# Copies of value pages into a DRAM scratch: all from SyncE beside the input projection, or shared out over SyncE and ScalarE and three stages

## What is computed

```python
for l in range(DEPTH):                        # 2
    h = x @ w_in                              # 1024 -> 2836 columns
    y_conv = conformer_conv(h_conv, ...)      # GLU, causal conv of width 31, LayerNorm, swish, pointwise
    y_pool = pool_mixer(h_pool, ...)          # causal window sums
    # past of the 8 decode sequences: 32 pages of 128 tokens each, rows [k_cmp, v_cmp, k_sel, v_sel]
    past = take(cache_nsa_kv[l, :, :, c], page_table)      # c = 0..3
    y_att = nsa_mixer(q, kv, gates, past, ...)             # compressed + selected + window branch
    y_gdn = gdn_mixer(...)                    # gated delta rule
    x1 = layer_norm(ALPHA * x + concat(...) @ w_out)
    x = layer_norm(ALPHA * x1 + square(relu(x1 @ w_up)) @ w_down)
```

## Time and profile before

| what | value |
|---|---|
| median of 3 runs | 3044.47 us |
| profiled execution, own time | 3055.84 us |
| its span | 3054.1 us |
| PE busy | 2617.3 us (86%) |
| DVE, ACT, POOL busy | 873.4, 568.4, 236.7 us |
| DMA queue q1 (SyncE's), share of 16 engines | 32.0% |
| DMA queue q10 (ScalarE's) | 1.2% |
| mean granted TensorE clock | 0.895 |
| copies into v_dram | 512 DMAs of 64 KB |

### The profile page before, as it was taken

The page is one execution under the profiler, slowest core; times in us unless marked ns, Lnnn a source line. Parts: engine busy times, 40 slices in busy tenths (PEclk is TensorE's granted clock), DMA queues, the critical chain, the costliest instruction groups (busy, mean ns, idle before and its releaser), DMA issues. The chain is left out here.

```text
span 3054.1 us, 44579 instructions
## 1 busy us (share of the span) xinstructions
PE 2617.3 (86%) x17428; PEld 2135.7 (70%) x17428; DVE 873.4 (29%) x1901; ACT 568.4 (19%) x1180; POOL 236.7 (8%) x328
## 2 busy tenths in 40 slices
PE   6765699977698999999966677998868989999997
PEld 4554588856585888888755556887657758888885
DVE  2712133364534210000117112334545332000002
ACT  0000233244310200000110013332442103000002
POOL 0500000000130100000005000000002101000000
PEclk8977899989785999999978787999887769999998
DMA  5343467633001134022053435775410020341220
GB/s 191 101 119 105 120 213 221 190 139 141 2 22 49 42 107 128 28 71 67 1 153 106 119 86 169 225 221 167 174 46 1 21 91 28 103 132 28 55 56 30
DMA packets 348209, 310.55 MB, mean 102 GB/s; under 512 B 61985, under 2 KB 339618, under 8 KB 343514
## 3 DMA queue, kind: packets, MB, share of 16 engines
q1 hardware_dynamic: 339880, 295.66, 32.0%
q10 hardware_dynamic: 8114, 11.97, 1.2%
HBM read 297.71 MB, written 51.72 MB: 114 GB/s over the span
## 5 line engine op out<-in xcount | busy, mean ns | idle before, releaser
L383 PE MATMUL psum<-xT,w_ring 128*128 128x272 f32 x1408 | 364.4, 424 | 159.6 <-DMA w_ring<-in_w_in 155.6
L2257 PE MATMUL psum<-xT,up_ring 128*128 128x272 f32 x2048 | 470.3, 392 | 0.0
L383 PEld LDWEIGHTS psum<-xT,w_ring 128*128 128x128 f32 x1408 | 290.7, 208 | 233.2 <-DMA w_ring<-in_w_in 162.9
L2257 PEld LDWEIGHTS psum<-xT,up_ring 128*128 128x128 f32 x2048 | 389.1, 190 | 80.3
L2276 PE MATMUL psum<-ff,HT 128*128 128x272 f32 x1536 | 353.6, 392 | 0.0
L2276 PEld LDWEIGHTS psum<-ff,HT 128*128 128x128 f32 x1536 | 291.8, 190 | 60.2
L1001 PE MATMUL psum<-cst,cache 128*128 128x128 f32 x1600 | 209.0, 286 | 16.6 <-DMA cache<-in_cache_nsa_kv 10.3
L1001 PEld LDWEIGHTS psum<-cst,cache 128*128 128x128 f32 x1600 | 179.0, 145 | 39.3 <-DMA cache<-in_cache_nsa_kv 11.6
L2120 DVE SCALAR_TENSOR_TENSOR xT<-xT,psum 128x544 f32<-128x544 f32 (+1 forms) x42 | 24.2, 584 | 529.6 <-PE psum L2276 441.6
L1031 PEld LDWEIGHTS psum<-chunks,W 64*128 64x128 f32 x2304 | 132.8, 189 | 16.8 <-ACT st_sel L1111 11.7
L1031 PE MATMUL psum<-chunks,W 64*128 64x128 f32 (+1 forms) x2304 | 139.4, 277 | 0.0
(11 more groups left out here) (428 smaller groups left out, 2996.5 us busy)
## 6 DMA issues: line engine op xcount, KB each, us to landing
cache<-in_cache_nsa_kv SPq DMA_DIRECT2D x512, 192.0 KB, 2.8
v_dram<-in_cache_nsa_kv SPq DMA_DIRECT2D x512, 64.0 KB
up_ring<-in_w_up SPq DMA_DIRECT2D x32, 1024.0 KB, 5.3
HT<-in_w_down SPq DMA_DIRECT2D x12, 2048.0 KB, 9.1
w_ring<-in_w_in SPq DMA_DIRECT2D x20, 1024.0 KB, 5.5
W<-v_dram SPq DMA_DIRECT2D x16, 1024.0 KB, 7.8
p_sel<-v_dram SPq DMA_DIRECT2D x16, 1024.0 KB, 7.0
HT<-in_w_out SPq DMA_DIRECT2D x8, 1024.0 KB, 5.8
```

The source lines that it names most:

```text
L383: last = pe.matmul(psum[0:w.shape[1], 2 * (t % 4) + h, 0:HALF], w, moving(k)[:, h * HALF:(h + 1) * HALF], start=(k == 0), stop=(k == kt - 1))
L2257: last = pe.matmul(psum[:, 2 * (t % 4) + h, 0:HALF], up_ring[:, g % 3, k, (t % 2) * P:(t % 2) * P + P], xT[:, k, half_of(h)], start=(k == ...
```

## The change

The 256 page copies of a layer are split: 144 from SyncE in `proj` (16 after each of the groups 2 to 10), 72 from ScalarE in `proj` (8 after each of the tiles 5 to 13, behind that tile's copy from PSUM), 24 from SyncE in `conv` behind the loads of `compression_loads` and ahead of the wait for the transposes, 16 from SyncE in `nat`, ahead of all that it does there. The counts awaited at the end of each stage follow.

```diff
+PAGES_PROJ_SP, PAGES_PROJ_ACT, PAGES_CONV, PAGES_NAT = 144, 72, 24, 16
-def value_pages(S, l, sp, first, n, sem):
+def value_pages(S, l, eng, kind, first, n, sem):
     io, half = S.io, NPG // 2
     for f in range(first, first + n, 8):
-        for j, page in enumerate(page_numbers(S, mybir.EngineType.SP, f // NPG, f % NPG, 8)):
+        for j, page in enumerate(page_numbers(S, kind, f // NPG, f % NPG, 8)):
             src = layer(io.cache_nsa_kv, l)[ds(page, 1)].rearrange("a t c k d -> (a t) (c k d)")
             at = f % NPG + j
-            sp.dma_start(io.v_dram[f // NPG, at // half, :, at % half, :], src[:, 3 * P:4 * P]).then_inc(sem, 16)
+            eng.dma_start(io.v_dram[f // NPG, at // half, :, at % half, :], src[:, 3 * P:4 * P]).then_inc(sem, 16)
...
     def sync(sp, s, g):
-        if 2 <= g < 10:
-            value_pages(S, l, sp, (g - 2) * NPG, NPG, s.values)
+        if 2 <= g < 11:
+            value_pages(S, l, sp, mybir.EngineType.SP, (g - 2) * 16, 16, s.values)
     def sync_end(sp, s):
-        sp.wait_ge(s.values, 16 * NB * NPG)
+        sp.wait_ge(s.values, 16 * PAGES_PROJ_SP)
+        sp.wait_ge(s.values_act, 16 * PAGES_PROJ_ACT)
+    def with_pages(i, then):
+        def run(act, s):
+            if then:
+                then(act, s)
+            value_pages(S, l, act, mybir.EngineType.Activation, PAGES_PROJ_SP + 8 * i, 8, s.values_act)
+        return run
+    for i in range(PAGES_PROJ_ACT // 8):
+        t = T_POOL + 1 + i
+        more[t] = with_pages(i, more.get(t))
...
@@ conv_and_pool
         def _(sp):
             compression_loads(S, l, sp, s)
+            value_pages(S, l, sp, mybir.EngineType.SP, PAGES_PROJ_SP + PAGES_PROJ_ACT, PAGES_CONV, s.values)
             sp.wait_ge(s.copied, 5)
...
+            sp.wait_ge(s.values, 16 * PAGES_CONV)
...
@@ natural_keys
         def _(sp):
+            value_pages(S, l, sp, mybir.EngineType.SP, NB * NPG - PAGES_NAT, PAGES_NAT, s.pages)
             sp.wait_ge(s.copied_act, QT + 1)
...
+            sp.wait_ge(s.pages, 16 * PAGES_NAT)
```

More of the change, by code:

```diff
@@ L572, in project_in @@
           lhsT, N_IN, evac_act, evac_dve, beside=keep_window, ready=1, on_dve=on_dve, more=more,
-          more_names=("values", "sigmoid", "placed", "taps", "moved", "packed", "psteps", "pooled", "g_taps", "g_conv", "g_kept", "g_swish"))
+          more_names=("values", "values_act", "sigmoid", "placed", "taps", "moved", "packed", "psteps", "pooled", "g_taps", "g_conv", "g_kept", "g_swish"))
 def page_numbers(S, engine, b, first, n):
@@ L701, in conv_and_pool @@
     names = ("turned", "copied", "stored", "mean", "centred", "squared", "var", "ln", "rstd", "normed", "swish", "linear",
-             "scaled", "pointwise", "out", "zero", "misc", "cmp")
+             "scaled", "pointwise", "out", "zero", "misc", "cmp", "values")
     with stage(nc, "conv", *names) as (block, s):
@@ L830, in natural_keys @@
     kvn = sb("kv_rows", [P, QT, 6 * P], ctx=ctx)
-    with stage(nc, "nat", "turned", "copied_act", "copied_dve", "gates", "stored", "values", "zero", "placed") as (block, s):
+    with stage(nc, "nat", "turned", "copied_act", "copied_dve", "gates", "stored", "values", "zero", "placed", "pages") as (block, s):
         @block.gpsimd
```

## The result

The changed kernel took 2908.95 us (median of 4 executions, 2904.36 to 2915.67) against 3046.94 us before (4 executions): ratio 0.9552, 95% interval [0.9521, 0.9584]. The forecast was 2904 us. Run again later it gave 2912.72 us, ratio 0.9562 [0.9526, 0.9598]. The profiled execution took 2915.67 us, for which the prediction had 2916; its span is 2913.8 us, 140.3 less than before. The interval of a ratio is some 0.3% wide to either side, about 10 us, so differences of a few us are read from the timelines and not from the medians.

What follows compares the result with a forecast made beforehand. SyncE's sequencer issuing page copies was taken to bound the projection. Terms of -95.8 and -91.9 us for it, plus 2 x 23.8 for conv and nat, made -140 us: 2904 us, own range 2888 to 2920, whole range 2886 to 2945.

Steps and rivals of the forecast that it cites:

- The bound: Projection: it goes at the pace at which one sequencer, SyncE's, issues page copies, 27.36 us for a group.
- SyncE in the projection: Two blocks of eight copies instead of four a group, 14.0 us; projection ends 95.8 and 91.9 us earlier in the layers.
- the stall: SyncE's first copies in the projection: one issue of 11.95 us during the window copies, assumed to stay in place.
- ScalarE: Projection: 7.5 us a block of eight copies, priced from window copies; a lag of 7.7 us, hidden by PSUM slack.
- Conv: Stage conv: three blocks, 20.0 us, between SyncE's last load and first store; 5.1 hidden, +14.9 us a layer.
- Nat: Stage nat: two blocks, 13.4 us, ahead of SyncE's stores, less its old wait: +8.9 us a layer.
- DMA engines: Projection: a group's packets take 10.9 us of all 16 engines, a share of 0.74 in 14.7 us, so it fits.
- The margin: DMA engines in the projection: the copies fit if packets don't get longer than by a third.
- The rule of the Trainium skill: Against the change: a second issuer saves only sequencer time, usually little; by it alone the sum would be near nothing.
- Rival (b): Projection: one descriptor path serves both sequencers and copies take turns; 11 us a layer gained, 3022 us; chance 0.07.
- The argument against (b) from the load of 1 MB: Issuing 1 MB of rows takes no longer than 64 KB, so the instruction's time is hardly the descriptor generator's.

Runs made afterwards that it cites:

- e1: The changed kernel with ScalarE's 72 page copies of a layer back on SyncE in the projection: 2986.27 us, ratio 0.9816 to the kernel before.
- e7: The kernel before, with eight pages copied by one DMA, in order without the page table: 2866.82 us, ratio 0.9394 to the kernel before.
- e6: The changed kernel without ScalarE's eight window copies (4 MB a layer left out): 2912.44 us in two executions.
- e2: The changed kernel with conv's 24 copies moved to SyncE in the projection, behind group 10's: 2878.61 us, ratio 0.9437 to the kernel before.
- e3: The changed kernel with nat's 16 copies moved to ScalarE in the projection, behind tiles 14 and 15: 2891.18 us, ratio 0.9477 to the kernel before.
- e8: The changed kernel with twice the bytes in each page copy, k_sel and v_sel in rows of 1 KB: 2919.69 us in two executions.

## Why the prediction was right

*The bound* was SyncE's issue of copies. e1 (one issuer, 77 us slower) and e7 (one issuer, fewer instructions, TensorE bound) show it from both sides. That the profiled execution was met to 0.3 us is luck: the projection gained 2.5 us more than foreseen, conv and nat cost 1.6 more, and the start 0.65, which nobody foresaw.

*SyncE in the projection*: 14.0 us a group foreseen, 14.3 measured; group 10's load at 184.2 foreseen, 184.12 measured, which is two errors that cancel (group 4's load came 2 us early, the six steps behind it took 2 us longer); last record at 226.1, measured 225.7. Both layers: -187.7 against -190.2 us. Taking two blocks off the stretch with the stall and leaving the stall was right (24.69 us; 26.9 foreseen), though the trace of before could not say what the stall was; e6 does.

*ScalarE*: I took 7.5 us a block and a lag of 7.7 us. A block takes 5.8 to 6.9 us with its register work (6.1 for the first, from the evacuation's end at 101.68 to 107.78), its instruction 0.507 us against SyncE's 0.493, and there is no lag: every evacuation is ended by TensorE. The window copies' 0.84 us was the wrong row for the price; SyncE's own copies were the nearer kind. It changed nothing, because the PSUM slack covered either value.

*Conv*: +14.9 a layer foreseen, +15.8 and +15.6 measured. 20.2 us lie between the last load's issue and the first store (20.0 foreseen); most of the rest are the loads themselves, in layer 1 12.9 us against 12.2 before. Their time differs from run to run (12.1 in e1, 13.2 in e2), so nothing is read from it. *Nat*: +8.9 foreseen, +8.9 measured twice. e2 gives the term of conv back (31.4 us in the timelines for two layers), e3 that of nat only in part (15.0 of 17.8), as told there.

*DMA engines*: 0.74 foreseen, 0.78 measured; the loads' landing rose from 5.5 to 7.0 us. The margin that I put on it, a third, is near what e8 found: at 1.37 times the share the first wait for weights appears. The reason given for it was not right, since a share of 1 is no ceiling of that column; what ran out in e8 was the time between a load's issue and its use.

*The rule of the Trainium skill* (DMA: Bandwidth & Descriptors, "Issuing engines are not separate DMA queues") says that DMAs from several engines interleave on the same 16 DMA engines, and that a second issuer saves only sequencer time, "usually small relative to the DMA itself". The traces agree with the first half in so far as the weights' landing, all from SyncE, rose from 5.5 to 7.0 us when ScalarE issued too. The second half does not carry over to these 64 KB copies: an issue took 0.8 us where SyncE's copies landed in 2.2 (page of the changed kernel), and since landings overlap and one sequencer's issues don't, the issue time was the whole bound, worth 77 us in e1.

Rival (b)'s time, 3022, was not seen: with both queues at work an instruction took 0.493 us on SyncE and 0.507 on ScalarE. The argument against (b) from the load of 1 MB was weaker than it looked, as e7's instruction of 1.309 us shows. That the queues share something shows only in e6, under 4 MB of the other queue's copies.

## What to carry to other kernels

When an engine waits for a load that lands soon after its issue (5.5 us here), look at what stands ahead of the issue in its queue and count DMA instructions, not bytes: here 0.8 us each. A second sequencer is worth having up to the pace of the engine that it feeds; put its issues in pieces shorter than one tile of its own duty, since the buffers downstream give only so many tiles of slack. And before moving copies into stages behind, fill the queue's idle time at the end of the stage that bounds: the same copies cost 24 us a layer in conv and nat and nothing there.

## What the runs showed of the hardware that was not expected

A queue's large copies can hold up another queue's issue: SyncE's DMA instruction of 0.493 us took 11.5 us while ScalarE had eight copies of 508 KB out, and at most 1.147 us without them (e6). The DMA engines' share can stand at 1.07 over 40 us with the granted clock at 1.00 and one wait of 0.52 us in the weight loads of the matmul stream beside it (e8). Eight pages in one DMA cost 1.5 us to issue against 6.4 in eight (e7). After an idle time of 16.30 us TensorE's transposes ran at the lower clock, 1.51 us for six instead of 0.84 (e3).
